# Which partition each token of an expert takes: ranks through a table of 64 places

## The reference

```python
weights = pg_top * pe_top / jnp.sum(pe_top, axis=-1, keepdims=True)
e_idx = g_idx * EXPERTS_PER_GROUP + j_idx
combine = jnp.sum(jax.nn.one_hot(e_idx, N_EXPERTS) * weights[..., None], axis=1)
for e in range(N_EXPERTS):
    act = jax.nn.silu(hf @ w_gate[e]) * (hf @ w_up[e])
    y = y + combine[:, e:e + 1] * (act @ w_down[e])
```

## Time and profile before

| what | value |
|---|---|
| median of 3 runs | 1322.46 us (1321.29 to 1322.61) |
| the profiled execution | 1320.31 us, span 1318.5 us |
| mean granted TensorE clock | 0.971 |
| busy: TensorE, VectorE, ScalarE, GpSimd | 93%, 42%, 23%, 19% of the span |
| moved by DMA | 213.03 MB, mean 162 GB/s |

### The profile page before, as it was taken

The page is one execution under the profiler, slowest core; times in us unless marked ns, Lnnn a source line. Parts: engine busy times, 40 slices in busy tenths (PEclk is TensorE's granted clock), DMA queues, the critical chain, the costliest instruction groups (busy, mean ns, idle before and its releaser), DMA issues.

```text
span 1318.5 us, 13442 instructions
## 1 busy us (share of the span) xinstructions
PE 1226.3 (93%) x5000; PEld 690.7 (52%) x5000; DVE 557.7 (42%) x1424; ACT 308.2 (23%) x725; POOL 246.6 (19%) x214
## 2 busy tenths in 40 slices
PE   7999999999989999999999899999999799887884
PEld 3555434455544444588874546677664454333342
DVE  2214493476547742209962367421223522321221
ACT  4223643433310001132032255200001211110010
POOL 6100023354500000081500020312200112211100
PEclk9999999999989999999999999999999889988898
DMA  9625113224265612403240202202266599999992
GB/s 326 114 72 128 64 63 66 96 81 144 79 210 190 223 64 97 139 22 128 77 172 8 64 1 65 69 0 64 65 274 262 203 365 402 408 408 404 406 386 54
DMA packets 92247, 213.03 MB, mean 162 GB/s; under 512 B 20185, under 2 KB 51305, under 8 KB 79847
## 3 DMA queue, kind: packets, MB, share of 16 engines
q1 hardware_dynamic: 78800, 191.53, 39.4%
q0 software_dynamic: 10176, 17.96, 5.7%
q10 hardware_dynamic: 3200, 2.61, 0.6%
HBM read 205.69 MB, written 14.75 MB: 167 GB/s over the span
## 4 chain that ended last, share of the span: by engine, by line
PE 75%; SPq 8%; DVE 7%; DMA 6%; ACT 2%; issue 2%; ACTq 0%; POOL 0%; POOLq 0%; DVEq 0%
PE PS L2276 7%; PE PS L991 6%; SPq L2762 6%; PE PS L634 5%; PE PS L1406 4%; PE PS L1484 4%; PE PS L2339 4%; PE PS L1667 4%; PE PS L1669 4%; PE PS L2445 3%; PE PS L2893 3%; DMA W<-in_w_up 2%; DMA AN<-in_w_down 2%; PE PS L1713 2%; PE PS L1415 2%; PE PS L1725 2%
## 5 line engine op out<-in xcount | busy, mean ns | idle before, releaser
L991 PE MATMUL PS<-HT,W 128*128 128x512 f32 x256 | 124.7, 610 | 1.8 <-ACT AN L1155 1.7
L1253 POOL TENSOR_SCALAR AN<-AN,SM 128x128 f32<-128x128 f32 (+3 forms) x64 | 72.3, 1137 | 198.5 <-DVE SM L1345 198.5
L1276 DVE SCALAR_TENSOR_TENSOR AN<-AN,COLA 128x256 f32<-128x256 f32 x168 | 85.3, 508 | 5.0
L2893 PE MATMUL PS<-AN,HT 128*64 128x512 f32 x192 | 61.8, 637 | 11.4 <-DMA AN<-in_w_up 6.2
L634 PE MATMUL PS<-W,HT 128*128 128x512 f32 (+1 forms) x192 | 70.9, 531 | 0.0
L2972 DVE TENSOR_TENSOR HT<-HT,PS 128x256 f32<-128x256 f32 x16 | 6.7, 422 | 150.9 <-ACT HT L2950 150.9
L991 PEld LDWEIGHTS PS<-HT,W 128*128 128x128 f32 x256 | 44.4, 193 | 39.0 <-issue 35.4
L1406 PE MATMUL PS<-HT,W 128*128 128x512 f32 x128 | 58.1, 599 | 0.0
L2445 PE MATMUL PS<-W,AN 128*128 128x512 f32 x128 | 57.6, 597 | 0.0
L1484 PE MATMUL PS<-W,AN 128*128 128x512 f32 x128 | 55.5, 593 | 1.9 <-DVE GBC L1290 1.9
L2339 PE MATMUL PS<-AN,W 128*128 128x512 f32 x128 | 55.7, 593 | 0.1
(11 more groups left out here) (511 smaller groups left out, 2277.5 us busy)
## 6 DMA issues: line engine op xcount, KB each, us to landing
W<-in_w_in SPq DMA_DIRECT2D x14, 2048.0 KB, 8.6
W<-in_w_down SPq DMA_DIRECT2D x20, 1024.0 KB, 21.7
AN<-in_w_ada SPq DMA_DIRECT2D x17, 1024.0 KB, 5.2
AN<-in_w_gate SPq DMA_DIRECT2D x17, 1024.0 KB, 20.7
AN<-in_w_up SPq DMA_DIRECT2D x17, 1024.0 KB, 23.5
AN<-in_w_down SPq DMA_DIRECT2D x12, 1024.0 KB, 22.9
W<-in_w_gate SPq DMA_DIRECT2D x10, 1024.0 KB, 20.9
W<-in_w_up SPq DMA_DIRECT2D x10, 1024.0 KB, 30.1
```

The costliest lines, as they stand in the source:

```text
L991: t = pe.matmul(u.ap, w[:, c, tile(m)], hT[:, c, :], start=c == 0, stop=c == 7)
L1253: pool.tensor_scalar(PU[u % 5][:, 0:n], PU[u % 5][:, 0:n], RSUM[:, u:u + 1], None, ALU.mult).then_inc(*sc_pool.up(u))
L1276: dve.scalar_tensor_tensor(out=a, in0=wt[:, c, :], scalar=ca["c2"][:, c:c + 1], in1=a, op0=ALU.mult, op1=ALU.add).then_inc(*ada_dve.up(p, c))
L2893: t = pe.matmul(u.ap[r, :].rearrange("p (n f) -> p n f", n=2), XGT[e % 2][:, c, r], w_gu(3 * e + half)[:, c], start=c == 0, stop=c == 7)
```

## The change

An expert's 64 places are taken in another order. A constant row `order` of 64 columns joins the table: `order[place] = rank`. Rank r goes to place `8 * (r % 8) + (r // 8 + 2 * (r % 8 // 2)) % 8`. So ranks 0 to 7 go to places 0, 8, 18, 26, 36, 44, 54 and 62. The comparison at L2639 reads `order` in place of `iota128`. `COLA` shrinks from 128 to 96 columns, which makes room for most of the new constant; the other SBUF buffers move by 128 or 256 bytes.

```diff
@@ constants() @@
     parts["iota128"] = np.broadcast_to(f, (128, 128))
+    order = np.empty(64)
+    for r in range(64):
+        order[8 * (r % 8) + (r // 8 + 2 * (r % 8 // 2)) % 8] = r
+    parts["order"] = np.broadcast_to(order[None, :], (128, 64))
@@ build() @@
-    COLA, COLB = sbuf("COLA", 128), sbuf("COLB", 128)
+    COLA, COLB = sbuf("COLA", 96), sbuf("COLB", 128)
@@ dve_place() @@
-        dve.tensor_tensor(RH[:, :, i, :], fv(k("iota128"), [[0, 2], [1, PLACES]]), fv(RNK[:, i:i + 1], [[4, 2], [0, PLACES]]),
+        dve.tensor_tensor(RH[:, :, i, :], fv(k("order"), [[0, 2], [1, PLACES]]), fv(RNK[:, i:i + 1], [[4, 2], [0, PLACES]]),
                           ALU.is_equal).then_inc(*rt_dve.up("oh", i))
```

## The result

The changed kernel takes 1309.69 us (median of 4 runs, 1308.09 to 1313.11) against 1322.49 us before (1321.29 to 1322.61). The medians are 12.8 us apart. The forecast was 1313.8, in a range of 1308.0 to 1319.5. The profiled execution took 1308.09 us, its span is 1306.3 us.

A forecast was written before the change was run, and what follows sets the result against it. One late DMA engine, with 102 rows against a mean of 64, was taken to bound the expert stage. Terms -8.8 + 0.4 - 0.3 = -8.7 us took 1322.46 to 1313.8 us, range 1308.0 to 1319.5.

The forecast's parts named there:

- The other two maps: Row-to-engine maps the prediction rejected from the last scatter's steps: eight neighbouring partitions to an engine, or partition modulo 16.
- The steps at zero: Larger constant, comparison, moved buffers and first gather each taken as 0; up to 0.1 us for the constant, 0.3 for buffers.
- The last landing: Arrival of the last down weights in the expert stage, forecast 8.8 us earlier, near 1294 us.
- the three ways of adding: Estimates for the last landing: 8.4 us with the factor, 11.3 without it, 6.2 if only the old lag was shortened.
- The factor of 0.74: Late engine's seen lag, 14.6 us, against 19.7 priced from its rows over the mean; also applied after the change.
- full price: Fullest engine's rows over the mean at 0.162 us per gathered and 0.338 per accumulated row, without the factor.
- What is late next: After the last landing: up to 0.4 us lost to TensorE's path from the last up weights, 0.3 gained in the last scatter.
- Rival A: TensorE's own chain takes over at the end: gain 5.4 + 0.3 us, time 1316.8 us; chance 0.14.
- B: Nearly even: engines ahead no longer run dry, gain 12 to 14 us, time about 1309.5 us; chance 0.12.
- C: Late engine is late for a reason of its own, not its rows: only noise, 1322.5 us; chance 0.05.
- D: Last engine of a half has its own burden, up to 11 us, hidden by few rows: 1322.4 us; chance 0.05.
- E: Same engine as D with more than 11.1 us of its own: slower, 1327 us at 16 us; chance 0.06.

The follow-up runs named there:

- the kernel packed by engine: Kernel before, with ranks 0 to 7 on all eight places of a half's first engine, ranks 8 to 15 on the second's, and so on: 1335.8 us, ratio 1.0107.
- back and forth: Kernel before, with a table whose groups of eight ranks take a half's eight engines in turn, every other group in reverse: 1310.18 us, ratio 0.9912.
- the move alone: Changed kernel with the comparison reading iota128 again, so old order of places but larger table and moved buffers: 1322.2 us, ratio 1.0007.
- the table alone: Kernel before with the new ranks in columns 64 to 127 of iota128, no buffer moved: 1309.35 us, ratio 0.9916; again 1311.08 us, ratio 0.9928.
- the packing from the other end: Kernel before, ranks packed as before but starting at each half's last engine, so the eighth has the 102 rows: 1321.68 us, ratio 1.0006.
- the swapped version: The back-and-forth table, with experts e and e+16 swapping halves in odd tiles: 1307.48 us, ratio 0.9896; again 1306.09 us, ratio 0.9897.

## Why the prediction was right

**The bound.** One late DMA engine set the end, and its rows made it late. This is shown: the stage kept its length when the same counts lay on other engines, grew by 13.9 us when rows were added to the fullest, and shrank as they were spread. The steps from 102 to 78 and from 78 to 67 rows are clear in the times too; the one at 73 rests on the stage of one profile.

**The map of partitions to engines**, read off the steps of one scatter, gives the order of the nine kernels in the table, with ties where the counts are equal. The other two maps are excluded by the kernel packed by engine, and again by back and forth: by them its fullest engine has 128 rows (before 128) or 87 (before 79), so no gain or a loss, and it gained 11 us. The Trainium skill's section "The descriptor swizzle" in "DMA: Bandwidth & Descriptors" gives this map for a transfer of 128 partitions. The indirect DMAs of this kernel, which skip rows, agree with it: 128 rows on the fullest engines cost 13.9 us more.

**The steps at zero.** The constant, the comparison, the moved buffers and the first gather: together nothing that can be told (ratio 1.0007, interval 0.9995 to 1.0019, so within some 2 us; 292 ns for the comparison in both; TensorE's wait for the first gather 4.6 us before and 4.7 after).

**The last landing.** Forecast 8.8 us earlier. The stage got shorter by 252.7 - 243.9 = 8.8 us in the two profiles compared; over the four profiles with this table (mean 244.0) by 8.7. The size is right, but part of its working is not, and that it came out to 0.1 us is luck: the three ways of adding gave 8.4, 11.3 and 6.2, and 8.8 was chosen near the first. The factor of 0.74 was fitted to one lag and applied to both sides. It holds from 102 to 78 rows (8.7 of 11.3 us at full price) and fails from 102 to 128 (13.9 of 13.0). The full price for an engine's own rows would fit an engine that is never without work. But this agreement may be in part chance: in the kernel packed by engine the packets of weights took 328 ns on average and not 313, and the trace doesn't say on which engines. From 78 to 67 rows the stage gets 4.8 us shorter, 0.44 for each row; from 102 to 78 it is 0.36. Why less is won there is not settled.

**The share and the landing.** The sign that was named, a share near 1 until 1285 us and then a fall in 8 us, came otherwise: it is 0.87 from 1278 to 1280 us, 13 us before the landing, and 0.11 in the last three. The landing was named for 1294 and came at 1290.95, of which 2.7 us are the earlier start of the stage.

**What is late next.** The 0.4 us given to TensorE were not due. Its last product still waits for the down weights, 1.35 us (1.05 before):

```profile
1284.52 3.67 PE L2887 MATMUL PS<-AN,HT 128*64 128x256 f32 x32 [1.15 <-DMA AN<-in_w_up]
1289.19 0.50 PE L2869 MATMUL PS<-K,HT 128*128 128x128 f32 x2 [1.00 <-DVE HT L2976]
1291.04 3.65 PE L2918 MATMUL PS<-AN,HT 128*64 128x512 f32 x16 [1.35 <-DMA AN<-in_w_down]
```

Rival A so did not come about. The last scatter gave 0.65 us with the rest of the tail, for 0.3 forecast.

**The sum and its remainder.** Forecast 8.7 us, measured 12.8 in the first comparison. Of the profiled 12.2 us, 8.8 are the stage, 0.65 the tail and 2.7 the time ahead of it. The last is noise between executions, as the move alone and the second profile of the changed kernel show; what makes the stage start earlier or later stays open. The later comparison of the same changed kernel gave 1321.36 - 1312.75 = 8.6 us, the table alone 12.0 and 9.6. So the first measurement lies at the fortunate side of what this change gives, 9 to 12 us. That "everything before 1050 us should agree within 0.3 us" was wrong: the stage starts anywhere from 1047.1 to 1051.3 us in these profiles, with nothing changed ahead of it.

**The rivals.** B (nearly even, 1309.5 us) lies nearest to the first median, but not by its mechanism: after the change the last landing is still 5.4 us behind the even end, and the version that is nearly even takes 1306.1 to 1307.5. C fell with the table alone. D and E fell with the packing from the other end for the last engine of the lower half, and with the swapped version, whose last landing is 1.5 us behind the even end, for that of the upper half. The Trainium skill, "DMA: Bandwidth & Descriptors", "Latency and other measured facts", says that DMA engines 7 and 15 are usually slower. By more than a microsecond or so in the 240 us of this stage that is not borne out here: the packing from the other end puts the 102 rows on the first of them for 0.7 us more, and the swapped version has 66 rows on each. The second was not tried with 102.

## What to carry to other kernels

When a stage is bound by DMA, look at how its share ends: a stretch at one sixteenth before the last landing means that one engine is late, and that no bandwidth is missing. Transfers that skip rows load the engines by partition, so fill the places in an order that goes round the engines, and count the rows per engine over the whole stage, not per transfer. Compare a gain of one per cent by the stage's own length, since the start of the stage moved by 4 us from one execution to another.

## What the runs showed of the hardware

- A row of 4 KB that is scattered with accumulation costs its DMA engine about twice a plain one: packets of 327 ns against 159 (medians), and leaving the accumulation out shortened the stage by 14.1 us where 15 were worked out.
- One late engine leaves the others at work for long: with 102 rows on the fullest, the mean share from 1080 to 1280 us was 1.02; with 128 on five engines it was 0.99, and the rate 379 GB/s in place of 405. That the others had then run out of issued loads is the likely reading.
- The last product of the kernel runs wholly or mostly at the lower clock level in some executions (5.24 to 5.37 us against 3.67, in 5 of 13 profiles), and in both ways with the same code.
